# Layer norm in a hybrid GLA / Gated DeltaNet step: 80 products of constants on TensorE in its waits

## What is computed

```python
def layer_norm(x, g, b):
    mu = jnp.mean(xf, -1, keepdims=True)
    var = jnp.mean(jnp.square(xf - mu), -1, keepdims=True)
    return ((xf - mu) * lax.rsqrt(var + LN_EPS) * g + b)
...
x = layer_norm(DEEPNORM_ALPHA * x + FFN_RES * swiglu_ffn(x, ...), ...)
x = layer_norm(DEEPNORM_ALPHA * x + y, ...)          # y: the mixer's output
```

## Time and profile before

| | us |
|---|---|
| median of 3 runs | 3205.69 (3202.62 to 3209.05) |
| the profiled execution | 3211.07 |
| its span, first to last instruction | 3209.0 |
| PE busy in the span | 3035.0 (95%) |
| mean granted clock of TensorE | 0.973 |
| DVE, ACT, POOL busy | 1344.0, 1010.5, 997.1 |

### The profile page before, as it was taken

The page is one execution under the profiler, slowest core; times in us unless marked ns, Lnnn a source line. Parts: engine busy times, 40 slices in busy tenths (PEclk is TensorE's granted clock), DMA queues, the critical chain, the costliest instruction groups (busy, mean ns, idle before and its releaser), DMA issues.

```text
span 3209.0 us, 61353 instructions
## 1 busy us (share of the span) xinstructions
PE 3035.0 (95%) x25670; PEld 2902.1 (90%) x25670; DVE 1344.0 (42%) x1911; ACT 1010.5 (31%) x1746; POOL 997.1 (31%) x412
## 2 busy tenths in 40 slices
PE   8999998998899999899999889999999888999997
PEld 8999997887899999899999888888988778999997
DVE  3212253335621313631222667776376656312126
ACT  2111126333331111432211355544354433321112
POOL 3333343221433333433333421111311104333332
PEclk9999998999899999999999889999999988999998
DMA  3222221222122222122222112121212111222222
GB/s 132 73 79 79 77 82 46 81 74 82 56 75 74 76 83 73 59 79 75 78 79 79 60 41 69 62 69 63 66 63 69 62 43 53 79 73 74 85 73 78
DMA packets 62315, 230.57 MB, mean 72 GB/s; under 512 B 8257, under 2 KB 10177, under 8 KB 58754
## 3 DMA queue, kind: packets, MB, share of 16 engines
q1 hardware_dynamic: 56898, 200.27, 19.0%
q10 hardware_dynamic: 5184, 26.74, 2.2%
HBM read 209.76 MB, written 17.22 MB: 71 GB/s over the span
## 4 chain that ended last, share of the span: by engine, by line
PE 69%; issue 21%; DVE 4%; POOL 4%; ACT 2%; POOLq 0%; DVEq 0%; ACTq 0%
PE gem L228 60%; PE gem L531 4%; POOL wl L283 3%; POOL xl L481 1%; PE msc L423 1%; PE msc L683 1%; PE msc L691 1%; DVE work L392 0%; PE msc L416 0%; PE msc L516 0%; ACT x L436 0%; DVE work L882 0%; DVE work L885 0%; ACT xh L434 0%; ACT small L1343 0%
## 5 line engine op out<-in xcount | busy, mean ns | idle before, releaser
L283 POOL TENSOR_TENSOR wl<-raw,wh 128x1024 fp32r<-128x1024 f32 x368 | 934.2, 2539 | 2112.1 <-ACT wh L246 2112.1
L246 ACT CAST wh<-raw 128x1024 fp32r<-128x1024 f32 x368 | 386.4, 1050 | 1424.0 <-PE gem L228 1402.3
L228 PE MATMUL gem<-xh,wh 128*128 128x320 f32 x2688 | 612.7, 309 | 5.0 <-POOL wl L283 5.0
L228 PE MATMUL gem<-xl,wh 128*128 128x320 f32 x2688 | 612.6, 309 | 0.0
L228 PE MATMUL gem<-xh,wl 128*128 128x320 f32 x2688 | 612.3, 309 | 0.0
L228 PEld LDWEIGHTS gem<-xh,wh 128*128 128x128 f32 x2688 | 449.0, 188 | 5.9 <-ACT work L329 5.4
L228 PEld LDWEIGHTS gem<-xh,wl 128*128 128x128 f32 x2688 | 449.5, 188 | 0.0
L228 PEld LDWEIGHTS gem<-xl,wh 128*128 128x128 f32 x2688 | 449.3, 188 | 0.0
L350 DVE TENSOR_TENSOR work<-work,gem 128x640 f32<-128x640 f32 x88 | 72.3, 821 | 877.8 <-PE gem L228 840.8
L228 PE MATMUL gem<-hh,wh 128*128 128x320 f32 x1792 | 408.8, 309 | 2.1 <-issue 2.1
L228 PE MATMUL gem<-hl,wh 128*128 128x320 f32 x1792 | 408.6, 309 | 0.0
(11 more groups left out here) (256 smaller groups left out, 2829.3 us busy)
## 6 DMA issues: line engine op xcount, KB each, us to landing
raw<-wstream SPq DMA_DIRECT2D x368, 512.0 KB, 3.5
work<-gdn_s ACTq DMA_DIRECT2D x8, 1024.0 KB, 4.9
gdn_s_out<-work ACTq DMA_DIRECT2D x8, 1024.0 KB, 4.0
work<-gla_s ACTq DMA_DIRECT2D x4, 1024.0 KB, 5.7
gla_s_out<-work ACTq DMA_DIRECT2D x4, 1024.0 KB, 3.9
x<-x_in SPq DMA_DIRECT2D x2, 1280.0 KB, 8.0
y_out<-x SPq DMA_DIRECT2D x8, 320.0 KB, 2.2
gdn_p_out<-work ACTq DMA_DIRECT2D x8, 128.0 KB, 4.1
```

The lines of the kernel that those rows point to most:

```text
L228: mm = pe.matmul(gem[:, par, s, 0:HALF], w, r[:, k, s * HALF:(s + 1) * HALF], start=(k == 0 and n == 0), stop=(k == kts - 1 and n == 2))
L246: act.copy(wh[:, par, :], raw[:, par, :]).then_inc(hi_ready.sem, hi_ready.by)
L283: pool.tensor_tensor(wl[:, par, :], raw[:, par, :], wh[:, par, :].bitcast(F32), ALU.subtract)\
```

## The change

`pe_ln` gets a helper that issues n matmuls of 192 columns, with `ident_r` as the weights and the first 192 columns of `cr` as the moving operand, both rounded to fp32r. They write columns 320 to 511 of the first bank of `gem` slot 0, which nothing reads. 16 stand before the wait for `zsum`, 18 before the wait for `zsqs`, 28 after the statistics, and 18 behind the broadcasts, but not in the last layer norm. Two waits are put before the first 16: for the rounded constants, and for the evacuation of the phase's last even tile from slot 0.

```diff
+        def idle_products(pe, n):
+
+            for _ in range(n):
+                pe.matmul(gem[:, 0, 0, HALF:HALF + 192], ident_r, cr[:].rearrange("p a n -> p (a n)")[:, 0:192],
+                          start=True, stop=True)
+
         def pe_ln(pe, ph):
             L = LN_OF[ph]
+            pe.wait_ge(rounded.sem, rounded.at(0))
+            pe.wait_ge(evacuated[0].sem,
+                       evacuated[0].at(half(base[PLAN[PLAN.index(ph) + 1]] if ph != PLAN[-1] else N_CHUNKS) - 1))
+            idle_products(pe, 16)
             for a, src in ((0, zsum), (1, zsqs)):
+                if a:
+                    idle_products(pe, 18)
                 pe.wait_ge(sum_ready.sem, sum_ready.at(KT * L + KT - 1, a))
                 for t in range(TT):
                     mm = pe.matmul(msc[:, 0, a * 8 + t:a * 8 + t + 1], src[:, t * P:(t + 1) * P],
                                    cs[:, C_MEAN:C_MEAN + 1], start=True, stop=True)
             mm.then_inc(stat_mm.sem, stat_mm.by)
+            idle_products(pe, 28)
             for j, (b, dg) in enumerate(((0, diag_r), (2, diag_n))):
                 flat = dg.rearrange("p t n -> p (t n)")
                 pe.wait_ge(diag_ready.sem, diag_ready.at(L, j))
                 for s in range(2):
                     mm = pe.matmul(msc[:, b + s, 0:HALF], ones, flat[:, s * HALF:(s + 1) * HALF], start=True, stop=True)
                 mm.then_inc(bc_ready.sem, bc_ready.by)
+            if ph != PLAN[-1]:
+                idle_products(pe, 18)
```

## The result

| | before | changed |
|---|---|---|
| median of 9 runs | 3209.05 us (3202.62 to 3216.12) | 3198.18 us (3197.52 to 3202.76) |
| profiled execution, span | 3211.07, 3209.0 us | 3202.18, 3200.2 us |
| mean granted clock | 0.973 | 0.985 |

The ratio of the changed kernel to the one before is 0.9973, with a 95% interval of 0.9963 to 0.9983. The kernel is faster, as forecast, but by 0.27% where the sum said 0.49% (3189.9 of 3205.69): nearly half of the gain is missing.

A forecast was written before the change was run, and what follows sets the result against it. TensorE, busy 3035.0 of 3209.0 us, was taken to lose time idle and at half clock in layer norms. Gains 13.0 + 0.3 + 2.5 = 15.8 us off 3211.07 give 3195.3, less 5.4 is median 3189.9; range 3184 to 3205.

The forecast's parts named there:

- the sum: Whole kernel: 13.0 us from five heads, 0.3 from the sixth, 2.5 from tails, 15.8 us off, median 3189.9.
- What bounds the kernel, and the mechanism: Layer norms: TensorE idles and drops to half clock; products of constants keep full clock, shortening statistics and broadcasts.
- Price of a product: Each added 192-column matmul: 0.09 us at full clock, bounds 0.06 and 0.15; 0.16 at half clock.
- Before `zsqs`: Between the statistics' halves: ten records and 18 products take 2.8 us, just inside the 2.88 us wait.
- The 28: Products after the statistics: with ten records 3.67 us against 3.46 for the diagonals, a cost of 0.2 us.
- In the sixth: Sixth layer norm, no wait for `zsqs`, 18 products paid in full: 9.0 us against 9.33, 0.3 us gained.
- Broadcast to add: From first broadcast to first add of a normed tile: 2.6 us at full clock, from 4.75 at half clock.
- Long head: First half of statistics to first add; forecast head, from the second half, 6.3 us, gaining 13.0 us over five.
- The tails: First add to end of first output tile: shrink to GpSimd's `xl` floor of 16.40 us, 2.5 us in all.
- The covers: First 16 (1.4 us) fit PE's 1.99 us idle wait; last 18 end 0.6 us before `xh` comes.
- The clock: Layer norm heads: stays at 1.00, margin thin; rivals: falls everywhere, 3221, chance 0.11; falls in some, 3200, 0.13.
- The mixers: Rival: waits in GLA and Gated DeltaNet swallow gains of first and fourth layer norms; 3196, chance 0.08.

The follow-up runs named there:

- experiment 2: The change with products of 256 columns into another bank, counts 17, 14, 19, 18, none between the halves in the sixth layer norm: 3190.08 us, ratio 0.9947.
- experiment 3: The change with products of 64 columns in place of 192, same counts: 3243.2 us, ratio 1.0104.
- experiment 1: The change with counts 16, 15, 20, 18 in place of 16, 18, 28, 18, none between the halves in the sixth layer norm: 3204.78 us, ratio 0.9973.
- experiment 5: The kernel of experiment 2 without the last 18 products behind the broadcasts: 3191.52 us, ratio 0.9953.
- experiment 6: The kernel of experiment 2 without the first 17 products, before the first half of the statistics: 3205.04 us, ratio 0.9993.
- experiments 9 to 16: Kernel before and changed kernel, both unchanged, profiled again; over all profiles Gated DeltaNet means 853.9 and 852.1 us, GLA 333.9 and 334.7.
- experiment 7: The kernel of experiment 2 with no products in the sixth layer norm: 3190.5 us, ratio 0.9944.
- experiment 8: The kernel of experiment 2 with no products in the fourth layer norm, before Gated DeltaNet: 3194.85 us, ratio 0.9962.

## Why the prediction was right or wrong

**What bounds the kernel, and the mechanism: right.** The clock was lost in the layer norms, the products held it in the head of each of the 36 that were profiled of the change, and the chain got shorter by broadcasts and statistics at full clock.

**Price of a product: this step failed.** The prediction took 0.09 us, between two rows. Measured are 0.114 us for 192 columns (485.10 to 488.29), inside its bounds of 0.06 and 0.15. A better row was at hand: 20 records of one column each took 2.39 us, 0.12 each, with next to nothing streamed. Ten records of 128 columns took 1.33 us, which tells the same. In the traces of before, the change and experiments 2 and 3, no stream of ten or more records with weights of 128x128 came faster than 0.10 us each at full clock: 64 columns cost nearly as much as 192, and at 256 (0.124) the columns begin to show. The 0.06 us was the distance between two single starts. The first of the two, L1113, was held back by the matmul of 512 columns before it, and its own weight load had begun 0.23 us earlier:

```profile
1902.83 0.19 PEld L1113 LDWEIGHTS msc<-cr 128*128 128x128 f32 x1
```

That such a single distance leaves out a weight load which each of 28 products in a row has to pay is the likely reason; no run tests it.

The Trainium skill ("TensorE: Matmul & The Clock Gate", section "LDWEIGHTS (loading the stationary operand)") gives P / 1.2 ns for a weight load of P columns, 107 ns for 128. At full clock the trace agrees with a pace set by that, 0.114. The 82.5 ns that the prediction worked out by the Trainium skill (same page, section "Back-to-back issue gap") was further off than its own 90: that section gives the formula for a matmul by itself and says that at few columns it leaves out the weight load. At half clock the pace was 0.213 with 64 columns and 0.218 with 192 (forecast: 0.16, by the column).

**What follows from it.** Before `zsqs`, 18 products and ten records take 3.21 us where 2.88 are free (forecast 2.8): 0.3 us late. The 28 end 0.9 us after the diagonals (forecast 0.2). In the sixth both are paid in full: 9.90 in place of 9.33, 0.6 us slower, where the forecast had 0.3 faster. Broadcast to add took 2.44 us (forecast 2.6). Long head forecast 2.88 + 6.3 = 9.2, measured 9.90; heads gave 8.9 us where 13.3 was forecast. With 0.114 in place of 0.09 the prediction's own sum has the second half 0.3 us and the 28 another 0.7 us later, five times, and 1.1 us in the sixth: 6.1 us less, and so 9.7 in place of 15.8, close to what was measured. The experiments bear it out: where the clock held with counts for the measured price, the long head is 8.9 us, with 192 columns (experiment 1, two layer norms) as with 256 (experiment 2, five). That the median of experiment 2, 3190.1, is the number forecast for the change is chance.

**The tails: right.** 2.8 us against 2.5, and all at GpSimd's floor, 16.25 to 16.41: PE waits for the last `xl` of the first tile at 506.39. In the second and third layer norm of this profile the clock fell again, for 3.4 us at 856.0 and 1340.7, and the tails are 16.41 all the same, as the prediction said of a short fall. Without the last 18 one tail of five was 0.7 us longer (experiment 5).

**The covers: right for the 16 and the last 18.** PE still waited 0.22 us for the first sum.

**The clock: right, near the edge as said, and helped by the wrong price.** Experiments 1 and 6 show how near: with three products fewer between the halves, or the first group left out, the clock falls in the heads of four and of all six layer norms. Had the 18 and the 28 been fitted to their waits at the right price, as in experiment 1, the clock would, going by that profile, not have held in all six. That part of the forecast came true with groups that overran their waits, which is luck.

**The mixers: 0.8 us in GLA, none in Gated DeltaNet that can be told from its scatter.** The 0.8 us come with the place of one half-clock stretch (experiments 9 to 16).

**The sum.** In the mean of the profiles (five and six) long heads and tails went from 151.8 to 141.1 us, 10.7 less; 0.8 back in GLA leaves 9.9. The two medians of 9 runs differ by 10.9 us and the ratio gives 8.7. The forecast was 15.8. It started from a median of 3205.69 us for the kernel before, and nine runs of it gave 3209.05.

## What to carry to other kernels

Products of constants can keep TensorE's clock up through a wait. Here 256 columns cost 9% more time than 192 and kept the clock with groups that end before the wait does, where 192 did so in some layer norms only; 64 columns cost nearly as much and lost it. Price such filler by the densest run of weight load and matmul pairs in the trace, not by its columns or by the distance of two single matmuls, and check each group against the wait it stands in. One that overruns is on the critical path, at nearly twice the price if the clock falls after all (0.218 against 0.114 us). Before blaming a change for a stage that it doesn't touch, profile both kernels several times more.

## What the runs showed of the hardware

- Pace of weight load and matmul pairs, fp32r, 128x128 weights: 0.114 us for 192 columns and 0.124 for 256 at full clock; 0.213 for 64 and 0.218 for 192 at half clock.
- A stream of such pairs with 64 columns and the statistics among them, without a gap for some 12 us, left the clock at 1.2 GHz; products of constants with 192 columns and the change's counts, or with 256 and fewer, held it at 2.4 GHz through the heads. With 256 that is so in all 19 heads profiled with all groups in front of the broadcasts (experiments 2, 5, 7 and 8); of three sixth layer norms without the group between the halves, one lost it. Three quarters of the elements of the wider ones are zeros, and nearly all of the narrow ones.
- With the same instructions the clock held in one layer norm and fell in another of the same execution (experiment 1: two and three of the first five).
- A stage that TensorE doesn't fill can differ by 12 us of 850 between executions of the same kernel (849.50 and 861.78 before), and the longest had most half clock (0.95 of the full clock over the stage).
